# A decoder block on eight cores: the last adaLN chunk, two x tiles and the q, k, v weights issued in order from GpSimd's queue, and eight steps of transposes moved from the DMA to TensorE

## The reference

```
ada = silu(c) @ w_ada + b_ada ; shift, scale, gate = split(ada, 3)
h = rms_norm(x, norm_g) * (1 + scale) + shift
z = h @ w_in                                     # 1024 x 8704, all branches at once
for g, (window, dilation) in ((128, 1), (512, 4), (2048, 16)):
    q, k = partial_rope(rms_norm(z_q)), partial_rope(rms_norm(z_k)) ; v = z_v
    o, lse = dilated causal attention (8 heads of 64)
attn = sum_g softmax(lse)_g * o_g ; y_a = attn * silu(z_gateA)
y_b  = u * (W_s @ layer_norm(v) + b) * silu(z_gateB)      # per 128-token chunk
out  = x + gate * ((sig(.) * y_a @ w_a + sig(.) * y_b @ w_b) @ w_out)
```

## Time and profile before

| | |
|---|---|
| median of 3 runs | 745.45 us (745.08 to 745.57) |
| the profiled execution | 745.08 us |
| its longest span (core 0, first to last instruction) | 743.5 us |
| spans of the other cores | 737.9 to 742.3 us |
| TensorE busy on core 0 | 699.5 us, 94% |
| VectorE, ScalarE, GpSimd busy | 63%, 48%, 40% |

### The profile page before, as it was taken

One profiled execution on the slowest core, in us unless ns is written; L12 is line 12 of the kernel. 1 busy time (PEld: TensorE's weight loads), 2 busy tenths in 40 slices (PEclk: granted clock), 3 DMA queues, 4 the chain that ended last, 5 costly groups with the idle time before them and its releaser, 6 DMA issues.

```text
span 743.5 us, 14552 instructions; the slowest of 8 cores (737.9 to 743.5 us)
## 1 busy us (share of the span) xinstructions
PE 699.5 (94%) x4560; PEld 357.2 (48%) x4638; DVE 471.5 (63%) x790; ACT 357.9 (48%) x679; POOL 296.1 (40%) x379
## 2 busy tenths in 40 slices
PE   7768999999999999999999999999999999999995
PEld 2434555445666654555554444444444444444442
DVE  6527799995688788898888864555844223222323
ACT  3626887767655555567666555564121111111110
POOL 1414234454445565443334003577243343343343
PEclk9759999999999999999999999999999999999998
DMA  8994114466465776541222508049960313121324
GB/s 243 319 182 140 58 58 115 68 97 108 73 86 80 95 81 74 86 63 29 32 30 35 102 1 142 1 72 179 202 208 22 114 57 114 56 60 56 113 59 169
DMA packets 71243, 72.10 MB, mean 97 GB/s; under 512 B 48640, under 2 KB 54912, under 8 KB 70912
## 3 DMA queue, kind: packets, MB, share of 16 engines
q1 hardware_dynamic: 51072, 40.49, 23.3%
q0 software_dynamic: 17648, 22.29, 21.4%
q10 hardware_dynamic: 2448, 8.39, 2.8%
HBM read 74.82 MB, written 8.39 MB: 112 GB/s over the span
## 4 chain that ended last, share of the span: by engine, by line
PE 68%; DVE 8%; ACT 6%; DMA 6%; issue 5%; SPq 3%; POOL 2%; DVEq 0%; ACTq 0%; POOLq 0%
PE ps L249 60%; DVE arena L258 8%; ACT arena L258 6%; DMA arena<-w_ada 3%; SPq L261 3%; DMA arena<-arena 2%; PE ps L662 2%; POOL arena L258 2%; PE ps L547 2%; PE ps L698 1%; PE ps L703 1%; PE ps L366 1%; SPq L611 0%; PE ps L620 0%; PE ps L1064 0%
## 5 line engine op out<-in xcount | busy, mean ns | idle before, releaser
L249 PE MATMUL ps<-arena 128*128 128x512 bf16 x2521 | 569.4, 380 | 12.3 <-DVE arena L258 4.6
L258 POOL TENSOR_TENSOR arena<-arena 128x128 bf16<-128x128 f32 (+5 forms) x308 | 257.6, 845 | 381.3 <-DVE arena L258 307.0
L249 PEld LDWEIGHTS ps<-arena 128*128 128x128 bf16 x2596 | 271.2, 107 | 284.4 <-issue 21.9
L258 ACT ACTIVATE arena<-ps 128x1024 bf16<-128x1024 f32 (+2 forms) x283 | 191.9, 708 | 245.8 <-PE ps L249 155.6
L258 DVE TENSOR_TENSOR arena<-ps,arena 128x512 bf16<-128x512 f32 (+2 forms) x214 | 166.3, 798 | 60.8 <-PE ps L249 24.5
L258 ACT ACTIVATE arena<-arena 128x8 f32<-128x8 f32 (+8 forms) x272 | 114.5, 432 | 86.0 <-DVE arena L258 58.8
L258 DVE SCALAR_TENSOR_TENSOR arena<-arena,ps 128x512 f32<-128x512 f32 x80 | 54.5, 687 | 111.1 <-PE ps L249 93.1
L258 DVE TENSOR_TENSOR arena<-arena 128x1024 bf16<-128x1024 bf16 (+5 forms) x111 | 78.6, 711 | 22.1 <-POOL arena L258 10.7
L258 DVE TENSOR_REDUCE arena<-arena 128x8 f32<-128x512 bf16 x96 | 65.0, 681 | 24.5 <-ACT arena L258 24.0
L258 DVE SCALAR_TENSOR_TENSOR arena<-arena 128x512 f32<-128x512 f32 (+3 forms) x40 | 33.2, 831 | 13.4 <-DMA arena<-w_ada 6.5
L258 DVE TENSOR_SCALAR arena<-arena 128x512 bf16<-128x512 bf16 (+5 forms) x57 | 27.7, 485 | 17.4 <-DMA arena<-arena 9.1
(11 more groups left out here) (42 smaller groups left out, 176.2 us busy)
## 6 DMA issues: line engine op xcount, KB each, us to landing
arena<-x SPq DMA_DIRECT2D x32, 512.0 KB, 4.8
arena<-w_in POOLq DMA_DIRECT2D x44, 256.0 KB, 4.8
arena<-w_ada SPq DMA_DIRECT2D x15, 512.0 KB, 14.6
out<-arena ACTq DMA_DIRECT2D x15, 512.0 KB, 5.0
arena<-w_in POOLq DMA_DIRECT2D x6, 1024.0 KB, 12.8
arena<-w_adag SPq DMA_DIRECT2D x8, 512.0 KB, 7.8
arena<-w_out POOLq DMA_DIRECT2D x2, 1024.0 KB, 22.5
arena<-arena SPq DMA_TRANSPOSE x78, 4.5
```

The source lines that it names most:

```text
L249: ins = e.matmul(out_ap, l, r, start=(i == 0), stop=(i == n - 1))
L258: P.op(eng, lambda e: getattr(e, meth)(*a, **kw), reads=reads, writes=writes)
```

## The change

Chunk 3 of w_ada no longer stands in SyncE's list. GpSimd issues it, gated on the landing of chunk 2's first piece, then the twelve weight pieces of group 0 with x4 behind the sixth and x5 behind the tenth. The weights' own gate falls away. x6 and x7 stay on SyncE. The 14 spins ahead of chunk 3's column become 19, in three portions that wait for pieces of chunk 3.

Eight transposes (four of q, four of k) stand between the v products and the next q products, as in steps 4 to 7; they wait for GpSimd's rotary. The diff:

```diff
--- before.py
+++ after.py
@@ -285,12 +285,13 @@
         wada = acc.rearrange("p a b c -> p (a b c)").rearrange("p (c k w) -> p c k w", c=4, k=8)
 
         def x_load(t, gate=(), q="sp"):
-            dma(q, xs[t % 4], x_d[t * 128:(t + 1) * 128, :], "xs%d" % (t % 4), reads=gate)
+            P.op(q, lambda e: e.dma_start(out=xs[t % 4], in_=x_d[t * 128:(t + 1) * 128, :]), reads=gate, writes=["xs%d" % (t % 4)],
+                 slot="x%s%d" % (q, t % 4))
 
         dma("sp", misc, misc_d, "misc")
         pieces = [[(0, 2), (2, 4), (4, 6), (6, 8)]] * 3 + [[(0, 2), (2, 4), (4, 6), (6, 7), (7, 8)]]
         for c in range(4):
-            for lo_, hi_ in pieces[c]:
+            for lo_, hi_ in pieces[c] if c < 3 else ():
                 dma("sp", wada[:, c, lo_:hi_, :], wada_d[:, c, lo_:hi_, :], "wada%d_%d" % (c, lo_))
             for t in ((0,), (1, 2), (3,), ())[c]:
                 x_load(t)
@@ -460,6 +461,8 @@
         rot_tables(0, "dve")
         rot_tables(2)
         rot_tables(1)
+        for lo_, hi_ in pieces[3]:
+            dma("pool", wada[:, 3, lo_:hi_, :], wada_d[:, 3, lo_:hi_, :], "wada3_%d" % lo_, reads=["wada2_0"])
         sq_own(0)
         x_prep(0)
         ada_row(1, 0)
@@ -495,21 +498,24 @@
             x_mods(kc, "act", 2, 2)
         for j in (0, 1, 2):
             for p_ in range(4):
-                load_w(j, 512 * j, p_, p_ + 1, ["wada2_6"])
-        for t in range(4):
-            x_load(t + 4, gate=[("ws0p2", "ws1p2", "ws2p1", "ws2p3")[t]])
+                load_w(j, 512 * j, p_, p_ + 1)
+                if p_ == 1 and j:
+                    x_load(j + 3, q="pool")
+        for t in (2, 3):
+            x_load(t + 4, gate=[("ws2p1", "ws2p3")[t - 2]])
         ada_sum(3, 4, 8)
-        spin(14, 7)
+        spin(7, 7, ["wada3_0"])
+        spin(7, 7, ["wada3_2"])
+        spin(5, 7, ["wada3_4"])
         ada_col(3)
         for kc in (6, 7):
             x_mods(kc, "act", 0, 2)
             x_mods(kc, "dve", 2, 2)
...
@@ -595,17 +601,14 @@
             X("pool", "tensor_tensor", ka + kb, keys, out=z3[:, :, 8:16], in0=a3[:, :, 8:16], in1=b3[:, :, 0:8], op=ALU.add)
 
         def kgain(s):
-            if 8 <= s < 47:
+            if 16 <= s < 47:
                 k_, g = "kr%d" % (s % NK), steps[s][0]
-                if s < 16:
-                    X("act", "activation", [k_, "gcol"], [k_], out=kr[s % NK], in_=kr[s % NK], func=AF.Copy, scale=gprod[:, g:g + 1])
-                else:
-                    X("dve", "tensor_scalar", [k_, "gcol"], [k_], out=kr[s % NK], in0=kr[s % NK], scalar1=gprod[:, g:g + 1], scalar2=None, op0=ALU.mult)
+                X("dve", "tensor_scalar", [k_, "gcol"], [k_], out=kr[s % NK], in0=kr[s % NK], scalar1=gprod[:, g - 1:g], scalar2=None, op0=ALU.mult)
 
         def transp(s, roles=(0, 1), tb=TB):
             g, blk = steps[s]
             q_ = qi(s)
-            if 8 <= s < 47:
+            if 16 <= s < 47:
                 for r in roles:
                     ring, n, k_ = ((qr, NQ, "qr"), (kr, NK, "kr"))[r]
                     P.op("sp", lambda e, r=r, ring=ring, n=n: e.dma_start_transpose(out=ring[s % n], in_=qn[q_][:, r, :]),
@@ -803,8 +806,6 @@
         def last(role):
             for s in range(4):
                 proj_part(s, role, 3)
-                if s == 3 and role == 1:
-                    transp(2, (0,), 2)
                 sumsq(s, role)
                 if s == 2:
                     rstd2(0, role)
@@ -816,6 +817,8 @@
                         rs_own(4)
                         sc_own(4)
                 if s == 3 and role == 1:
+                    proj(4, 0)
+                    transp(2, (0,), 2)
                     sq_own(5)
                     rs_own(5)
             rstd2(2, role)
@@ -828,13 +831,12 @@
         phase(1, 0)
         phase(1, 1)
         x_load(8)
+        phase(1, 2)
         x_transp(4, TH)
         x_mod(4, TH)
-        phase(1, 2)
         for s in range(2):
             transp(s, (0,), s)
         last(1)
-        proj(4, 0)
         sumsq(4, 0)
         phase(2, 0, range(3))
         phase(2, 1, range(3))
@@ -842,9 +844,9 @@
         x_load(9)
         rstd(4, 0, 8)
         scaleqk(4, 0)
+        phase(2, 2, range(3))
         transp(0, (1,), 3)
         transp(1, (1,), 4)
-        phase(2, 2, range(3))
         for s in range(3):
             proj_part(s, 2, 3)
             vevac(s, "act" if s == 1 else "dve")
@@ -865,8 +867,6 @@
         fin_at[47] = (0, 2)
         for it in range(4, NS):
             a, b_, c_ = it - 1, it - 3, it - 4
-            if 8 <= a < 16:
-                transp(a)
             if it > 4:
                 proj(it, 0)
                 sumsq(it, 0)
@@ -913,14 +913,14 @@
             accum(c_, 1)
             proj(it, 2)
             vevac(it)
-            if not 8 <= a < 16:
-                transp(a)
+            transp(a)
             if it + 3 < NT:
                 x_sq(it + 3, ssqk[qi(it + 1)][:, 16:17], "ssq%d2" % qi(it + 1))
-            if 8 <= it < 12:
-                load_w(3, 3072, it - 8, it - 7)
-            for n in (range(2), range(2, 5), range(5, 8))[it - 12] if 12 <= it < 15 else ():
-                load_w(4 + n // 4, 3584 + 512 * (n // 4), n % 4, n % 4 + 1)
+            if it == 8:
+                load_w(3, 3072)
+            if it == 13:
+                load_w(4, 3584)
+                load_w(5, 4096)
             if it == 16:
                 dma("sp", svc, bsp_d, "bsp")
             if 17 <= it < 29:
```

More of the change, by code:

```diff
@@ L196, in build_nc @@
     gcol = small[:, 60:66]
-    gprod = small[:, 76:79]
+    gprod = small[:, 66:68]
     lngh = small[:, 68:72]
@@ L508, in build_nc @@
         g2_ = gqk.rearrange("p (g r) -> p g r", r=2)
-        X("dve", "tensor_tensor", ["misc"], ["gcol"], out=gprod, in0=g2_[:, :, 0], in1=g2_[:, :, 1], op=ALU.mult)
+        X("dve", "tensor_tensor", ["misc"], ["gcol"], out=gprod, in0=g2_[:, 1:3, 0], in1=g2_[:, 1:3, 1], op=ALU.mult)
         for b0 in (0, 64):
-            X("dve", "memset", [], ["gcol"], small[b0:b0 + 16, 60:66], 1.0)
-            X("dve", "memset", [], ["gcol"], small[b0:b0 + 16, 76:79], 1.0)
+            X("dve", "memset", [], ["gcol"], small[b0:b0 + 16, 60:68], 1.0)
         TB = 3
```

## The result

The changed kernel takes 740.18 us in the median (739.25, 740.18 and 740.66), against 745.45 for the kernel before on the same chip: a ratio of 0.9928, 95% interval 0.9906 to 0.9951. The forecast was 740.8, faster. (In some executions all cores of a die run at a lower clock; one of four is of that kind on either side, and such runs are left out of every time and ratio here.) The profiled execution took 739.25.

What follows compares the result with a forecast made beforehand. TensorE was taken as the bound, busy 94% of 743.5 us, with waits mainly at the head. 745.08 - 3.2 - 1.5 - 0.5 + 0.6 = 740.5, with the median's 0.37 near 740.8; range 737.3 to 745.4.

Steps and rivals of the forecast that it cites:

- Chunk 3's way: Head: chunk 3 issued near 26.0, moving near 30.3, complete between 38 and about 40; products 3.2 us earlier.
- Spins and clock: Before the column: 19 spins take 4.3 us at the low clock, ending at 45.4, or 43.3 at the high clock.
- the nearer bound of 44.2: Head: the q products start between 44.2 and 47.2, taken as 45.5.
- deeper gain: Rival: chunk 3 complete at 38, x3 not halved, clock high before the column, full steps at 7.95; 737.6 us, chance 0.17.
- the clock term: First q products: clock rising near 44 to 46 saves 1.5 us, bounds 0 and 1.9.
- Two microseconds of margin and more everywhere: Head: q, k and v weights land before their products, so x4 and x5 between weights cost nothing.
- Moved transposes: Head: moving transposes of x4, q2, k0 and k1 covers three waits, 3.1 us together; 0.5 kept, bounds 0 and 1.5.
- The loop: Steps 9 to 16: transposes back on TensorE, next weights in whole transfers; costs core 0 0.6 us, bounds -0.3 and 1.6.
- no change: Rival: x3 late and cold spins hold the column until 47.2, every full step takes 8.26; 745.2 us, chance 0.17.
- slower: Rival: GpSimd's queue takes nearly all the engines, chunk 2's last piece lands at about 39; 748.3 us, chance 0.08.

Runs made afterwards that it cites:

- the head part alone: The change's new transfer order, spins and moved transposes, with DMA transposes and weight pieces of steps 8 to 15 as in the kernel before: 741.95 us, ratio 0.9958.
- the whole-transfer kernel: Against the head part alone: DMA transposes kept only in steps 8 to 11, and the next weights sent in whole 1 MB transfers: 745.67 us, ratio 1.0021.

## Why the prediction was right, and where its steps were not

On core 0 the profiled spans go from 743.5 to 737.7: 5.40 by the earlier start of the q products, 1.69 between there and the first second product, against 0.88 more in steps 9 to 16 and 0.47 in the rest. The forecast was 3.2, 2.0 and 0.6.

Core 0 flatters the head. In that one execution of the kernel before its products started later than on any other core: at 48.70, the others between 43.53 and 46.93. The 6.25 us of idle time in the earlier trace rows are 3.13 on core 3 of the same execution:

```profile
43.29 1.84 PE L408 MATMUL ps<-arena 128*128 128x1 f32 x8 [3.13 <-DVE arena L258]
44.99 12.39 PE L547 MATMUL ps<-arena 128*128 128x512 bf16 x48
```

On the mean of the eight cores the products start at 45.9 before and at 42.4 after (42.3 in the change run again), 3.5 earlier, and the first second product gains another 1.6; steps 9 to 16 take 63.86 before and 63.63 after, 0.2 less. So 3.2 and 2.0 were near what the change does to a core, and 5.40 is what it did to the latest one. Core 0 isn't slow by its program: in the 55 executions of the kernel before that stand beside the experiments it is the slowest core in 9, and every core is in at least 5. The metric is the greatest of eight spans that change places from one execution to the next; the prediction made its sum on one of them.

**Chunk 3's way.** The issue came at 27.25, not 26, and the first bytes 2 to 3 us later instead of 4.3; the two errors cancel, and q0 starts at about 30 as forecast. By the figure of the Trainium skill ("DMA: Bandwidth & Descriptors", "Latency and other measured facts") it would have started near 28 (an estimate); the trace is between the two. The step that failed is what q1 had left then. I took 1.7 us for chunk 2's last piece and 1.6 for x3, 1.03 MB at 0.311 MB per us; it had 0.26. I had read a piece's landing as if all its bytes were that far back. The earlier trace rows had the better figure: of the 3.72 MB left at 26, chunk 3 is 2.1, and 4.3 us at 0.311 MB per us take 1.34 of the other 1.62, which leaves 0.28. q1's packets thin out (79, 40 and 9 in the windows above) while x3 lands only at 34.56; that a few engines were behind the others then is likely and not shown. So chunk 2 wasn't slowed (summed by 34.4 without an extra wait), and x3 came at 34.6 instead of 36.9. With x3 the transposes and the spins moved forward by 2.25 us.

**Spins and clock.** I took 4.3 us for the 19 spins at the low clock. The clock rose during them, at 40.8, and they took 3.27; the column fell from 1.84 to 1.02. Together with x3 this puts the first product at 43.30, 0.9 ahead of the nearer bound of 44.2: the start was mis-sized by 2.2. The rival "deeper gain" was nearer with x3 and with a clock that is high before the column; chunk 3 itself was complete at 40.51, not at its 38. VectorE, which I expected to be the earlier one, is 0.13 behind the spins (42.06 and 41.93). A product now takes (1.67 + 10.52) / 54 = 0.226 us against 12.21 / 47 = 0.260, over 47 of them 1.6, as the clock term said (1.5). It is not so on every core and in every execution, as the spins showed.

**Weights.** "Two microseconds of margin and more everywhere" was wrong at one place. The second q piece landed at 45.25, 2.7 us behind the first, and with the start 2.2 us earlier than forecast that is the wait of 0.41. x4 and x5 between the weights were booked at nothing; they gain: run without them there, the kernel is 2.4 us slower.

**Moved transposes.** x4's wait of 1.11 is gone, but 0.65 and 0.51 stand behind it; what remains fits the 0.5, and the runs can't tell it from nothing.

**The loop.** Steps 9 to 14 at 8.26 and 7.95, step 15 at 7.51 (I took 7.65), no DMA wait in them: right. Step 16, 8.06, has a wait I had excluded: the second of two transfers of 1 MB landed 16.64 us after its issue (13.6 on core 1), where I took 12 for both. Without the wait the step takes 7.60, against 7.15 before between the same products: 0.45 more, near my 0.4. Core 0's cost of 0.88 is within the bounds (which, worked out again from the term's own figures, are -0.4 and 1.5). But the term has the wrong sign in the time of the whole. Core 0 was the slowest in the execution that I read; in the head part alone it is one that stalls in step 15 (core 1), and taking the DMA transposes of steps 12 to 15 out of it gains another 2.5 us by the ratios (0.9958 and 0.9924). I had seen that core 4 "falls further", and not that on the repaired head this is what the metric gets.

**The sum.** That 740.8 came so near to 740.18 is luck in part. On core 0 the head gained 7.1 where I had 5.2, and the loop and the rest gave back 1.35 where I had 0.6: 5.7 for 4.6, in the fastest of the three executions. The loop part, which I booked as a cost, is what keeps a stall on another core from taking part of this gain; without it the time was 741.95.

The rivals: no change (745.2) and slower (748.3) are excluded by the interval, and the deeper gain's 737.6 lies just outside it. The slower one's mechanism was seen (q0 with 96.6% of the engines at 32.3 to 33.3), without its harm, since q1 was nearly done. The Trainium skill ("DMA: Bandwidth & Descriptors", "Queues, rings and completion order") says that each engine takes turns between its queues; shares of 62.9 to 39.5% in the first window fit that, and in the later ones q1 had too few packets left to tell.

What stays open: the 0.47 us in the rest of core 0, which is within what the cores differ there (556.0 to 558.6 after; one candidate, not tested, is a granted clock of 0.81 for 10.4 us from 520.1 on, against 4.8 us from 532.5 on before), and why the same two transfers of weights take longer on some cores and executions than on others.

## What to carry to other kernels

Where several transfers are wanted in an order, issue them in that order on one queue, each with its own semaphore: here it beat a gate by 2.8 to 3.4 us, and two queues with the late tile on the other by 2.4. Where the time is the greatest of several cores, make the sum on all of them, and in more than one execution; an edit that costs the slowest core of one profile 0.9 us was a gain of 1 to 3 us on the metric. Look at how many bytes a queue has left, not at when its last piece lands, to judge what a second queue will do to it.

## What the hardware showed that was not expected

- The DMA transposes of a step's q and k land with the weights issued beside them: 4.3 us from issue beside 0.25 MB, 8.3 beside 0.75, 11.3 beside 1 MB, and 2.5 with none beside them (core 1 of the whole-transfer kernel, 134 to 137). The Trainium skill ("DMA: Bandwidth & Descriptors", "Rules for kernel authors") says that a transpose next to ordinary DMAs needs nothing, in a rule on keeping transposes uncorrupted; for their time the runs show a price. Whether it is the bytes or the packets (1.05 MB in 144 packets for a whole transfer, 0.52 MB in 288 for two quarters) no run separates.
- After a stall of 3.12 or 4.51 us the next eight products took 3.6 us instead of 1.9, at a granted clock of 0.50: in these two cases the stall cost some 1.7 us more than itself.
